# Later transfers for the mixed groups, and the latents of layer 2 turned by VectorE, in a two-layer kernel

## What is computed

```python
q_lat, kv_lat = z[..., 3072:3584], z[..., 3584:3840]     # two latents of z = h @ w_in_2
q  = rmsnorm_2(q_lat, q_norm_2) @ w_uq_2                 # the latents feed two more products
kv = rmsnorm_2(kv_lat, kv_norm_2) @ w_ukv_2
m  = sigmoid(gate_a) * (ya @ w_branch_a_2) + sigmoid(gate_b) * (yb @ w_branch_b_2)
x  = x + m @ w_out_2                                     # "mixed groups": m, 512 columns at a time
x  = x + (silu(h2 @ w_gate_2) * (h2 @ w_up_2)) @ w_down_2
```

## Time and profile before

| | us |
|---|---|
| median of three runs | 2373.63 |
| the profiled execution | 2370.55 |
| its span, from the first to the last instruction | 2368.8 |
| TensorE busy in it | 2354.6 (99%) |
| VectorE busy | 1399.9 (59%) |
| ScalarE busy | 1186.1 (50%) |
| GpSimd busy | 59.4 (3%) |
| granted TensorE clock, mean | 0.999 |

### The profile page before, as it was taken

How to read it: one execution, slowest core, us unless ns; L and a number is a source line. 1 busy time by engine, 2 the same in 40 slices (tenths; PEclk the granted TensorE clock), 3 DMA queues, 4 the chain that set the end, 5 groups by cost and what they waited for, 6 DMA issues and landing times.

```text
span 2368.8 us, 29833 instructions
## 1 busy us (share of the span) xinstructions
PE 2354.6 (99%) x10552; PEld 1949.5 (82%) x10552; DVE 1399.9 (59%) x1586; ACT 1186.1 (50%) x1465; POOL 59.4 (3%) x94
## 2 busy tenths in 40 slices
PE   9999999999999999999999999999999999999998
PEld 7788888888888888888888888878888888888887
DVE  6786465676776765555565554766555555554544
ACT  6445455666666544445455554544544444444443
POOL 0000000000000000001130000000000000000000
PEclk9999999999999999999999999999999999999999
DMA  9776477788787766666787666666777777767664
GB/s 304 195 216 192 153 225 209 215 227 220 202 226 219 206 219 201 201 203 195 210 215 209 181 175 197 200 202 208 230 204 200 209 203 204 209 199 220 194 195 153
DMA packets 490442, 488.24 MB, mean 206 GB/s; under 512 B 248304, under 2 KB 275568, under 8 KB 490224
## 3 DMA queue, kind: packets, MB, share of 16 engines
q1 hardware_dynamic: 467888, 482.85, 69.5%
q10 hardware_dynamic: 22464, 4.20, 0.9%
HBM read 448.12 MB, written 2.10 MB: 190 GB/s over the span
## 4 chain that ended last, share of the span: by engine, by line
PE 96%; SPq 1%; DVE 1%; DMA 1%; ACT 0%; issue 0%; POOLq 0%; POOL 0%; DVEq 0%; ACTq 0%
PE acc L754 31%; PE acc L756 31%; PE acc L755 31%; SPq L382 1%; PE pair_banks L923 1%; DMA w_raw<-in_w_branch_a 1%; DVE w_lo L1447 0%; PE bank L942 0%; ACT w_hi L1081 0%; DMA w_raw<-in_w_in 0%; PE pair_banks L972 0%; PE pair_banks L895 0%; PE acc L780 0%; PE acc L784 0%; PE acc L787 0%
## 5 line engine op out<-in xcount | busy, mean ns | idle before, releaser
L1447 DVE TENSOR_TENSOR w_lo<-w_raw,w_hi 128x1024 fp32r<-128x1024 f32 (+1 forms) x842 | 1024.1, 1220 | 934.8 <-ACT w_hi L1081 933.2
L1081 ACT ACTIVATE w_hi<-w_raw 128x1024 fp32r<-128x1024 f32 (+1 forms) x842 | 886.0, 1055 | 1077.1 <-PE acc L756 980.9
L754 PE MATMUL acc<-w_hi,xT 128*128 128x512 f32 (+1 forms) x2208 | 861.4, 390 | 0.0
L756 PE MATMUL acc<-w_hi,xT 128*128 128x512 f32 (+1 forms) x2208 | 856.8, 388 | 0.0
L755 PE MATMUL acc<-w_lo,xT 128*128 128x512 f32 (+1 forms) x2208 | 856.7, 388 | 0.0
L754 PEld LDWEIGHTS acc<-w_hi,xT 128*128 128x128 f32 x2208 | 414.5, 188 | 87.1 <-issue 2.7
L756 PEld LDWEIGHTS acc<-w_hi,xT 128*128 128x128 f32 x2208 | 414.5, 188 | 85.4
L755 PEld LDWEIGHTS acc<-w_lo,xT 128*128 128x128 f32 x2208 | 414.6, 188 | 83.8
L754 PE MATMUL acc<-w_hi,f_hi 128*128 128x512 f32 x688 | 267.6, 389 | 0.0
L755 PE MATMUL acc<-w_lo,f_hi 128*128 128x512 f32 x688 | 267.6, 389 | 0.0
L756 PE MATMUL acc<-w_hi,f_lo 128*128 128x512 f32 x688 | 267.6, 389 | 0.0
(11 more groups left out here) (211 smaller groups left out, 1217.4 us busy)
## 6 DMA issues: line engine op xcount, KB each, us to landing
w_raw<-in_w_up SPq DMA_DIRECT2D x264, 512.0 KB, 4.2
w_raw<-in_w_in SPq DMA_DIRECT2D x198, 512.0 KB, 4.3
w_raw<-in_w_down SPq DMA_DIRECT2D x176, 512.0 KB, 4.5
w_raw<-in_w_gate SPq DMA_DIRECT2D x88, 512.0 KB, 3.7
w_raw<-in_w_out SPq DMA_DIRECT2D x64, 512.0 KB, 4.3
w_raw<-in_w_branch_a SPq DMA_DIRECT2D x16, 512.0 KB, 4.5
w_raw<-in_w_branch_b SPq DMA_DIRECT2D x16, 512.0 KB, 4.4
halves<-stage SPq DMA_DIRECT2D x234, 32.0 KB, 2.7
```

What stands on the lines that cost most here:

```text
L754: pe.matmul(o, l, w_hi[:, slot, k, 0:width], start=start, stop=False)
L756: last = pe.matmul(o, m, w_hi[:, slot, k, 0:width], start=False, stop=stop)
L1081: act.activation(in_slot(w_hi, slot, width), in_slot(w_raw, slot, width), ACT.Copy).then_inc(w_split_hi, 1)
L1447: dve.tensor_tensor(in_slot(w_lo, slot, width), in_slot(w_raw, slot, width), in_slot(w_hi, slot, width).bitcast(F32), ALU.subtract).then_i ...
```

## The change

```diff
@@ plan(), latents (the same for "ckv" behind group 42)
-    put(b + 1, "turn_lat", "cq", len(groups) - 1)
-    put(b + 2, "split_lat", "cq"); put(b + 2, "lat_rstd", "cq")
+    put(b + 1, "lat_blocks", "cq", len(groups) - 1)
+    for part in range(4):
+        put(b + 2 + part, "move_lat", "cq", part)
+    put(b + 13, "split_lat", "cq"); put(b + 2, "lat_rstd", "cq")
@@ plan(), mixed groups
-        for part in range(4) if n < 3 else (None,):
-            put(b + (part or 0), "move_mix", n, part)
+        for part in range(3) if n < 3 else (None,):
+            put(b + 2 + (part or 0), "move_mix", n, part)
         if n == 3:
-            put(b + 1, "move_mix_rest", n)
-        put(b + (7 if n < 3 else 3), "split_mix", n)
+            put(b + 2, "move_mix_rest", n)
+        put(b + (7 if n < 3 else 5), "split_mix", n)
@@ SP
+        def thirds(part):
+            return range(SP_SHARE) if part is None else range(6 * part, min(6 * part + 6, 16))
-                            move_mix(sp, args[0], shares(args[1]))
+                            move_mix(sp, args[0], thirds(args[1]))
+                        elif step_ == "move_lat":
+                            move_lat(*args)
+            def move_lat(kind, b):
+                k, _, blocks_, moved, _, _ = latents(kind)
+                sp.wait_ge(lat_blocks, k + 1)
+                for a_ in range(4):
+                    move_block(sp, moved, blocks_, b, a_).then_inc(lat_moved[k], 16)
@@ TensorE: on_turn_stage, on_turn_lat removed
-                    need = {0: (split_lo, lats[0])}
+                    need = {0: (lat_low, 1)}
@@ ScalarE, split_lat
+                k, nq, _, _, o, gain = latents(kind)
+                act.wait_ge(lat_moved[k], 256)
+                for q in range(nq):
+                    last = act.activation(o[:, 0, q].rearrange("p (n k) -> p n k", n=2 * 4), turned_latent(kind, q), ACT.Copy,
+                                          scale=cols[:, gain + q:gain + q + 1])
+                last.then_inc(lat_high, 1)
@@ VectorE
+            def on_lat_blocks(kind, g):
+                _, nq, blocks_, _, _, _ = latents(kind)
+                dve.wait_ge(acc_taken[g % 2], 2 * (g // 2 + 1))
+                for t in range(NT):
+                    last = dve.transpose(blocks_.rearrange("p (t b q k) -> p t q b k", t=NT, b=4, q=nq)[:, t],
+                                         stage[:, g % 2, t, 0:nq * P])
+                last.then_inc(lat_blocks, 1)
```

More of the change, by code:

```diff
@@ L162, in plan @@
     put(b, "evac", "stage", len(groups) - 1); put(b + 1, "lat_square", "cq", len(groups) - 1)
-    put(b + 1, "turn_lat", "cq", len(groups) - 1)
-    put(b + 2, "split_lat", "cq"); put(b + 2, "lat_rstd", "cq")
+    put(b + 1, "lat_blocks", "cq", len(groups) - 1)
+    for part in range(4):
+        put(b + 2 + part, "move_lat", "cq", part)
+    put(b + 13, "split_lat", "cq"); put(b + 2, "lat_rstd", "cq")
     b = group("w_in_2", 3584, 320, whole, "x")
     put(b, "evac", "ckv", len(groups) - 1); put(b + 1, "lat_square", "ckv", len(groups) - 1)
-    put(b + 1, "turn_lat", "ckv", len(groups) - 1)
-    put(b + 2, "split_lat", "ckv"); put(b + 2, "lat_rstd", "ckv"); put(b + 1, "rope", "kr", len(groups) - 1)
+    put(b + 1, "lat_blocks", "ckv", len(groups) - 1)
+    for part in range(4):
+        put(b + 2 + part, "move_lat", "ckv", part)
+    put(b + 13, "split_lat", "ckv"); put(b + 2, "lat_rstd", "ckv"); put(b + 1, "rope", "kr", len(groups) - 1)
     put(b + 4, "turn_kr"); put(b + 5, "copy_kr")
@@ L365, in two_layer_kernel @@
         p_blocks, p_moved = sem("p_blocks"), sem("p_moved")
+        lat_blocks, lat_high, lat_low = sem("lat_blocks"), sem("lat_high"), sem("lat_low")
+        lat_moved = [sem("cq_moved"), sem("ckv_moved")]
         mix_blocks, mix_moved = sem("mix_blocks"), sem("mix_moved")
@@ L403, in move_mix, with latents, turned_latent @@
             move_blocks_of(queue, which, flat_half, flat_stage[1], mix_moved)
+        def latents(kind):
+            if kind == "cq":
+                return 0, 4, over_y[0][:], over_y[4][:], cqT, G_CQ
+            return 1, 2, over_y[1][:, 0:CW], over_y[1][:, CW:2 * CW], ckvT, G_CKV
+        def turned_latent(kind, q):
+            _, nq, _, moved, _, _ = latents(kind)
+            return moved.rearrange("p (n q k) -> p n q k", n=2 * 4, q=nq)[:, :, q]
         def p_source(which, pair):
@@ L731, in _ @@
             chunk, group, splits, copies = Count(), Count(), Count(), Count()
-            rels, atts, pvs, lats = Count(), Count(), [0], []
+            rels, atts, pvs = Count(), Count(), [0]
             roped_n, turned_any = [0], []
@@ L976, in on_pool_y @@
                     free[2 + w] = (split_lo, splits.now)
[L978 to L988, removed]
             def on_turn_kr():
@@ L1007, in _ @@
                     "pv": on_pv, "pool_d": on_pool_d, "pool_y": on_pool_y,
-                    "turn_lat": on_turn_lat,
                     "turn_kr": on_turn_kr, "turn_kn": on_turn_kn}
@@ L1051, in _ @@
                 elif name == "w_uq_2" and col == 0:
-                    need = {0: (split_lo, lats[0])}
+                    need = {0: (lat_low, 1)}
                 elif name == "w_ukv_2" and col == 0:
-                    need = {0: (split_lo, lats[1])}
+                    need = {0: (lat_low, 2)}
                 elif name == "w_branch_a_2" and col == 0:
@@ L1231, in on_split_lat @@
             def on_split_lat(kind):
-                o, gain = (cqT, G_CQ) if kind == "cq" else (ckvT, G_CKV)
-                for b in range(2 if kind == "cq" else 1):
-                    high([o[:, 0, 2 * b], o[:, 0, 2 * b + 1]], b, gain + 2 * b)
+                k, nq, _, _, o, gain = latents(kind)
[4 more added lines that the diff above has]
+                last.then_inc(lat_high, 1)
             def on_split_mix(n):
@@ L1584, in on_split_pool @@
                     low([y_lo[:, k], y_lo[:, k + 1]], [y_hi[:, k], y_hi[:, k + 1]], 2 + w, G_POOL + k)
-            def on_split_lat(kind):
-                o, gain = (cqT, G_CQ) if kind == "cq" else (ckvT, G_CKV)
-                for b in range(2 if kind == "cq" else 1):
-                    low([o[:, 1, 2 * b], o[:, 1, 2 * b + 1]], [o[:, 0, 2 * b], o[:, 0, 2 * b + 1]], b, gain + 2 * b)
+            def on_lat_blocks(kind, g):
[5 more added lines that the diff above has]
+                last.then_inc(lat_blocks, 1)
+            def on_split_lat(kind):
+                k, nq, _, _, o, gain = latents(kind)
+                dve.wait_ge(lat_high, k + 1)
+                for q in range(nq):
+                    lo_, hi_ = (o[:, n, q].rearrange("p (n k) -> p n k", n=2 * 4) for n in (1, 0))
+                    last = dve.scalar_tensor_tensor(lo_, turned_latent(kind, q), cols[:, gain + q:gain + q + 1],
+                                                    hi_.bitcast(F32), ALU.mult, ALU.subtract)
+                last.then_inc(lat_low, 1)
             def on_split_mix(n):
@@ L1709, in _ @@
                     "select": on_select, "mask": on_mask, "norm": on_norm, "split_y": on_split_y, "split_x": on_split_x,
-                    "split_pool": on_split_pool, "split_lat": on_split_lat, "split_mix": on_split_mix, "res": on_res,
+                    "split_pool": on_split_pool, "lat_blocks": on_lat_blocks, "split_lat": on_split_lat, "split_mix": on_split_mix, "res": on_res,
                     "rstd": on_rstd, "lat_rstd": on_lat_rstd, "mix_a": on_mix_a, "mix_b": on_mix_b,
```

## The result

The changed kernel takes 2377.96 us (median of 17 runs, 2376.34 to 2380.62), the kernel before 2371.89 us (17 runs, 2370.63 to 2374.58): ratio 1.0025 [1.0018, 1.0033], slower by 6.07 us. The profiled execution takes 2376.34 us with a span of 2374.6, 5.8 us more than before.

The account below looks back on a forecast made before the run. TensorE, busy 99% of the span, was taken as the bound: latents -1.31, mixed groups through chunk 554 +4.0, slow issues +0.7, together +3.4 us on 2373.63, giving 2377.0 us; range 2371.0 to 2381.5.

Parts of the forecast that it names:

- Latents, -1.31 and no wait: Latents: twelve transposes leave TensorE, -1.31 us; late weight loads on SP cause no wait, at worst 1 us.
- Transfers start at M + 6.85, not M + 3.97: Mixed groups: SP's transfers start 2.9 us later, counted from M, when VectorE begins a group's gate product.
- The copies at b+7 wait, and close the loop: Groups 0 to 2: ScalarE's split_mix copies wait for transfers; the split of b+11 and next M stand behind.
- The loads are not the limit: Groups 0 to 2: weight load b+11 leaves at M + 15.2 and lands at M + 19.7, before the transfers.
- M' = M + 23.9: Groups 0 to 2: transfers landed at M + 20.4, next gate product at M + 23.9; 2.1 us lost per group.
- rival 2: Mixed groups' transfer chain: 24.6 us per group, ten transfers meet one slow issue; +5.5 us, 2379.1; chance 0.22.
- 0.7 us: Allowance in the sum for slow transfer issues in the longer chain, taken from between 0 and 1.4 us.
- Group 3, chunk 554 at M3 + 15.7: Last mixed group, w_out_2: TensorE begins chunk 554 15.7 us after group 3's gate product, +4.0 us against before.
- The clock: TensorE behind the 5 us wait for chunk 554: a fall to half rate would cost about 1.5 us; left out.
- Rival 1: The clock falls behind the wait for chunk 554: +4.9 us, 2378.5; chance 0.18.
- Rival 3: Mixed groups' chains never bind; both old TensorE waits and the transposes go: -5.6 us, 2368.0; chance 0.12.
- Rival 4: Mixed groups: landing takes 1.9 us, no slow issue; +0.3 us, 2373.9; chance with its neighbours 0.10.

Follow-up runs that it names:

- latents_only: Only the new latents, mixed groups as in the kernel before: 2370.42 us against that kernel's 2371.92, ratio 0.9994.
- three_later: Changed kernel with the transfers of mixed groups 0 to 2 one chunk later still (b+3 to b+5): 2382.63 us, ratio 1.0045 to the kernel before.
- split_one_later: Changed kernel with split_mix of groups 0 to 2 at b+8, not b+7: 2375.5 us, ratio 1.0016 to the kernel before.
- last_group_early: Changed kernel with mixed group 3 alone put back to its old places: 2373.35 us, ratio 1.0005 to the kernel before.
- five_parts: Changed kernel with groups 0 to 2 sent in five parts from b+1, split at b+8, group 3's SP transfers at b, split b+3: 2371.06 us, ratio 0.9998.

## Why the prediction was right or wrong

Forecast: +3.4 us, 2377.0, "same" with 0.48 as the likeliest. Measured: +6.1 us, 2377.96, slower by 0.25%. The time lies in the range and within 1 us of the forecast, but that flatters it: the three runs I started from (2373.63) stood 1.7 us above the median of 17, which made up for most of the 2.7 us by which the difference was too small. And by the prediction's own border of 0.2% the result lies just beyond it, in "slower" (0.40), though the interval [0.18%, 0.33%] reaches over the border.

- **Latents, -1.31 and no wait.** Right. Measured -1.36 in the pair of profiles, -1.5 in `latents_only`. The late loads were there (loads 396 to 399 left at 1098.27, 1101.45, 1105.52 and 1108.69) and ate cover, not time: the split of chunk 398 ended some 2.2 us ahead of TensorE, nearly 6 before.
- **Transfers start at M + 6.85, not M + 3.97.** Right: M + 6.63. Moving them by two chunks bought SP nothing. `three_later` moved them by another 2.3 us and M' by 1.9.
- **The copies at b+7 wait, and close the loop.** Right in mechanism: four waits of 2.7 to 5.2 us on ScalarE. "The loads are not the limit" held for this kernel but by a margin of only about 1 us; `split_one_later` ran straight into them.
- **M' = M + 23.9.** Mis-sized: 24.28 on the mean, between the forecast and rival 2's 24.6. All of it is in the issue and landing, at M + 20.8 and not M + 20.4; the step from the copies to M' was 3.47 (forecast 3.5). Packs of six transfers took 4.09, 4.59 and 4.45 us instead of 3.78 through single slow issues. For these I had added 0.7 us; they came to 1.1 in the loop.
- **Group 3, chunk 554 at M3 + 15.7.** Right: 15.87. The TensorE waits forecast as 1, 1.8 and 5 us were 1.67, 2.01 and 4.94.
- **The clock.** This is the step that failed. I left its 1.5 us out of the sum, with a chance of 0.18, because it had held through a wait of 2.5 us. It fell behind the 4.94 us wait at the price worked out (4.20 - 2.72 = 1.5 us). The Trainium skill's rule (TensorE: Matmul & The Clock Gate, "Why this matters for your kernels"), that a longer idle gap sends the clock back to half rate, agrees with this fall. It does not foretell the others: the clock also fell behind waits of 2.00, 2.01, 2.04 and 2.18 us in other profiles, and there the measurements decide. With the fall the sum was +4.9, against 5.8 in the pair; the remaining 0.9 is the slow issues beyond my 0.7 (0.4), group 3 (0.2) and the start of the kernel (0.3).
- **Rivals.** Rival 1 took place, together with half of rival 2. They were not alternatives but terms of one sum; a longer wait makes both likelier. Rival 3 fell: the transfers can't start before VectorE has made chunk b+5. Rival 4 fell: in the loop the landing took no less than 2.7 us.

Open: what decides whether the clock falls behind a wait of 2 to 2.5 us and how long it stays low, and how many falls the usual execution has beside the one of the profile.

## What to carry to other kernels

Where an in-order queue paces a loop, a step put later has to be followed to the next beginning of that same step: if what consumes it stays where it is, the wait only changes its name. Look for the resource that all the near-equal chains leave from (here SP's issue time, 16 x 0.64 us and the loads between, in a group of 21.8 us); rearranging on it moved the time by -2.8 to +11 us (1.5 us of gain from the latents included), relieving it removed every wait of the stage. And where the sum makes a wait longer than any the trace shows, the clock's fall belongs into the sum.

## What the runs showed that was not expected

- The clock fell behind waits of 2.01 and 2.18 us, though it had stood through 2.48 and 2.51 us in other kernels of this case. In `three_later` it fell behind 2.04 us (chunk start 1545.15) and held behind 2.04 us (1571.17) in one execution; a wait of 2.51 us before chunk 553 was followed by a fall in `last_group_early` and by none in `latents_only`. A chunk then ran at 0.43 us per matmul instead of 0.227.
- The landing of the same 32 KB transfer went with what the queue had issued ahead of it: 1.9 us far from a load, 2.7 close behind one, 4.06 with two loads among the eight issues ahead (`five_parts`; some 3.5 and 3.1 in its other two groups).
- Now and then a single transfer issue takes far longer than the usual 0.64 us: a pack of six came to 4.59 us instead of 3.78 with nothing else different in the queue.
